# Forming the sums and differences of the mix weight rows on GpSimd in three passes instead of on VectorE in two

## What is computed

```python
mod_x = (silu_c @ w_ada[i] + b_ada[i])[:, None, :]          # six vectors of 2048: shift, scale, gate, twice
hx = _modulate(x, g_norm_mix[i], sh1, sc1)                   # rms norm, scale, shift
f = jnp.fft.fftn(hg, axes=(1, 3), norm='ortho').real         # over the tokens and over 4 groups of 512 channels
ox = f.reshape(b, n, d) @ w_out                              # the mix weights, 2048 x 2048
x = x + ga1 * ox
x = x + ga2 * _sq_relu_mlp(_modulate(x, g_norm_ffn[i], sh2, sc2), w_ffn_in[i], w_ffn_out[i])
return _rmsnorm(x, g_final)
```

## Time and profile before

| | |
|---|---|
| runs | 1649.15, 1648.82, 1647.47 us |
| the profiled execution: span from first to last instruction | 1651.0 us |
| TensorE busy | 1606.8 us (97%) |
| VectorE busy | 1266.2 us (77%) |
| ScalarE busy | 545.4 us (33%) |
| GpSimd busy | 16.8 us (1%) |
| mean granted TensorE clock | 0.992 of full |

### The profile page before, as it was taken

One profiled execution on the slowest core, in us unless ns is written; L12 is line 12 of the kernel. 1 busy time (PEld: TensorE's weight loads), 2 busy tenths in 40 slices (PEclk: granted clock), 3 DMA queues, 4 the chain that ended last, 5 costly groups with the idle time before them and its releaser, 6 DMA issues.

```text
span 1651.0 us, 18364 instructions
## 1 busy us (share of the span) xinstructions
PE 1606.8 (97%) x7009; PEld 1235.1 (75%) x7009; DVE 1266.2 (77%) x1168; ACT 545.4 (33%) x659; POOL 16.8 (1%) x30
## 2 busy tenths in 40 slices
PE   6989999999999999999999999999999999999997
PEld 5653332688888888888888888888888888888875
DVE  6758996748888888886868686868677777777878
ACT  5420002453333333333333333333333333333332
POOL 0000000100000000000000000000000000000000
PEclk9999999999999999999999999999999999999998
DMA  9999997924544444342323233323223323333352
GB/s 355 362 409 342 410 340 271 351 97 129 177 132 174 135 171 146 135 128 79 124 85 118 92 111 101 102 102 102 102 102 102 102 102 102 102 102 102 103 203 102
DMA packets 96970, 272.64 MB, mean 165 GB/s; under 512 B 4332, under 2 KB 5660, under 8 KB 85020
## 3 DMA queue, kind: packets, MB, share of 16 engines
q1 hardware_dynamic: 93664, 249.91, 42.3%
q0 software_dynamic: 3120, 22.07, 3.8%
q10 hardware_dynamic: 144, 0.07, 0.0%
HBM read 263.64 MB, written 8.39 MB: 165 GB/s over the span
## 4 chain that ended last, share of the span: by engine, by line
PE 87%; DVE 8%; DMA 3%; issue 2%; ACT 1%; SPq 0%; DVEq 0%; ACTq 0%
PE banks L1307 16%; PE banks L1308 16%; PE banks L1309 16%; PE banks L1613 11%; PE banks L1615 11%; PE banks L1617 11%; DMA raw<-in_w_ada 2%; DVE acc_s L823 1%; DVE acc_a L823 1%; DVE acc_b L1020 1%; PE banks L1534 1%; PE banks L1325 1%; DVE mixw L921 1%; DMA mixw<-in_w_mix 1%; PE banks L1450 1%
## 5 line engine op out<-in xcount | busy, mean ns | idle before, releaser
L1146 DVE TENSOR_TENSOR stp<-raw,stp 128x1024 fp32r<-128x1024 f32 x330 | 402.0, 1222 | 154.9 <-ACT stp L690 152.2
L690 ACT ACTIVATE stp<-raw 128x1024 fp32r<-128x1024 f32 x330 | 343.0, 1054 | 521.7 <-PE banks L1309 231.3
L1307 PE MATMUL banks<-acts,stp 128*128 128x512 f32 x1024 | 399.7, 390 | 0.0
L1308 PE MATMUL banks<-acts,stp 128*128 128x512 f32 x1024 | 398.4, 389 | 0.0
L1309 PE MATMUL banks<-acts,stp 128*128 128x512 f32 x1024 | 398.4, 389 | 0.0
L1613 PE MATMUL banks<-stp,hid 128*128 128x512 f32 x840 | 326.8, 389 | 0.0
L1615 PE MATMUL banks<-stp,hid 128*128 128x512 f32 x840 | 326.8, 389 | 0.0
L1617 PE MATMUL banks<-stp,hid 128*128 128x512 f32 x840 | 326.8, 389 | 0.0
L1167 DVE TENSOR_TENSOR dacc<-dacc,banks 128x1024 f32<-128x1024 f32 x202 | 245.5, 1215 | 14.2 <-PE banks L1617 14.2
L1309 PEld LDWEIGHTS banks<-acts,stp 128*128 128x128 f32 x1024 | 192.2, 188 | 40.0
L1307 PEld LDWEIGHTS banks<-acts,stp 128*128 128x128 f32 x1024 | 192.3, 188 | 39.8 <-DVE stp L1146 0.4
(11 more groups left out here) (190 smaller groups left out, 1227.1 us busy)
## 6 DMA issues: line engine op xcount, KB each, us to landing
raw<-in_w_ada SPq DMA_DIRECT2D x80, 1024.0 KB, 8.2
raw<-in_w_ffn_in SPq DMA_DIRECT2D x64, 1024.0 KB, 7.3
raw<-in_w_ffn_out SPq DMA_DIRECT2D x64, 1024.0 KB, 5.1
mixw<-in_w_mix SPq DMA_DIRECT2D x16, 1024.0 KB, 10.3
gate_w<-in_w_ada POOLq DMA_DIRECT2D x16, 1024.0 KB, 5.3
xres<-in_x SPq DMA_DIRECT2D x4, 1024.0 KB, 9.0
xmix_d<-xres POOLq DMA_DIRECT2D x4, 1024.0 KB, 12.7
xmix<-xmix_d SPq DMA_DIRECT2D x4, 1024.0 KB, 8.0
```

The lines of the kernel that those rows point to most:

```text
L690: nc.scalar.activation(stp[:, slot, 0, :, :], source.rearrange("p (a n) -> p a n", a=2), ACT.Copy).then_inc(w_hi, 1)
L1146: nc.vector.tensor_tensor(stp[:, slot, 1, :, :], source.rearrange("p (a n) -> p a n", a=2), stp[:, slot, 0, :, :].bitcast(F32), ALU.subtra ...
L1307: nc.tensor.matmul(bank, w_hi_ap, m_hi, start=first, stop=False)
L1308: nc.tensor.matmul(bank, w_hi_ap, m_lo, start=False, stop=False)
```

## The change

`mix_sums` moves from DVE to GpSimd. [...] A pass waits for the one before it (`w_sum`), and the first for the tile's load. GpSimd does all 16 units in one loop, after the memset of `acc_s` and its bias row's DMA, and ahead of the memset of `acc_a`. On DVE the two passes of each unit are gone, and ahead of the first `up_low` stands a wait for `w_lo` at 16, which keeps the semaphore's count in order.

```diff
-    AHEAD = UPDATED[-1] + 1
@@ gpsimd
+            def mix_sums(n):
+
+                tile = mixw[n % MIX_SLOTS]
+                pool.wait_ge(mix_full[n % MIX_SLOTS], 16 * (n // MIX_SLOTS + 1))
+                nc.gpsimd.tensor_tensor(tile[:, 2:4, :], tile[:, 0:2, :], tile[:, 2:4, :],
+                                        ALU.subtract).then_inc(w_sum, 1)
+                pool.wait_ge(w_sum, 2 * n + 1)
+                nc.gpsimd.tensor_tensor(tile[:, 0:2, :], tile[:, 0:2, :], tile[:, 0:2, :],
+                                        ALU.add).then_inc(w_sum, 1)
+                pool.wait_ge(w_sum, 2 * n + 2)
+                nc.gpsimd.tensor_tensor(tile[:, 0:2, :], tile[:, 0:2, :], tile[:, 2:4, :],
+                                        ALU.subtract).then_inc(w_lo, 1)
+
             for i, acc in enumerate((acc_s, acc_a)):
                 if i == 0:
                     pool.wait_ge(chan_sum, 2 * GROUPS)
                 else:
+                    for n in range(MU):
+                        mix_sums(n)
                     pool.wait_ge(col_sum, 2)
@@ vector
-            def mix_sums(n):
-                ...
-            mix_sums(0)
             shift_vector()
@@ vector, the loop over the units
-                if 1 <= n < AHEAD:
-                    mix_sums(n)
...
-                if n == AHEAD - 1:
-                    for later in range(AHEAD, MU):
-                        mix_sums(later)
...
+            dve.wait_ge(w_lo, MU)
+
             def up_low(m):
```

## The result

| | before | changed |
|---|---|---|
| median of the runs | 1648.99 us (4 runs, 1647.47 to 1650.82) | 1690.40 us (4 runs, 1688.76 to 1691.21) |
| span of the profiled execution | 1651.0 us | 1687.9 us |
| GpSimd busy | 16.8 us | 186.4 us |
| VectorE busy | 1266.2 us | 1303.9 us |

The ratio is 1.0247, 95% interval 1.0232 to 1.0261: the change makes the kernel slower by 41.4 us, where 52 had been forecast. Between the two profiled executions the difference is 36.9 us. The span of an execution is about 1.9 us shorter than its time (1687.9 against 1689.83 us for the changed kernel's profiled one), so the profiled execution of the kernel before was some 3.9 us longer than its median and the changed one 0.6 us shorter; that is the 4.5 us between 41.4 and 36.9.

A forecast was written before the change was run, and what follows sets the result against it. The prediction took PE as the bound, with DVE and DMA close. DVE's 93.3 us and POOL's 94.5 us in turn made 187.8 against 145.6, +52.0 including 9.8 at the start; 1648.8 + 52 gave 1701 us, range 1676 to 1726.

The forecast's parts named there:

- one after the other: DVE's two-SBUF-operand passes and POOL's reading passes alternate in the full stretch: +52.0 us, chance 0.52.
- What bounds the kernel: Stage from 131.4 to 277.1 us: PE first, sums of units 2 to 15 hidden behind its about 10 us a unit.
- A pass on POOL: One GpSimd sum pass over 1024 elements a partition: 2.25 us, between 1.80 and 2.70; 7.35 us a unit with gaps.
- The start: Unit 0 has no cover: its sums ready on POOL at 123.0 us, so PE starts 9.8 us later.
- the ISA instruction: Unnamed instruction opening POOL's loop, ahead of the passes: taken at 5.2 us, between nothing and 10.3.
- Do they disturb each other: Whether DVE's gemv-stage passes and POOL's passes of 14 units slow each other: from 0 to +52.0 us.
- the high end: Full stretch: DVE's 93.3 us plus POOL's 94.5 make 187.8 where there were 145.6; +52.0 us with the start.
- Costed at nothing: DVE passes with one operand in PSUM or only one operand, 10.1 us in all, can go beside POOL's.
- The end: Late tile of w_ada, unit 15: PE's wait and slow clock, 6.5 us, stay since its load follows DVE's last passes.
- Side by side: Rival: the two engines do not disturb each other; 9.8 us lost, 0.9 + 6.5 back, 1651 us; chance 0.22.
- Half way: Rival: path shared in small pieces, or POOL's passes fall partly into DVE's gaps; about 1676 us; chance 0.13.
- Worse than the sum: Rival: PE waits each unit, its clock falls, units at half clock outlast POOL's; over 1726 us; chance 0.05.

The follow-up runs named there:

- the version with unit 15 later: Kernel before, all sums on DVE, those of unit 15 moved behind the combination and update of column block 2: 1644.73 us, ratio 0.9958.
- the thirty passes: Kernel before plus thirty GpSimd passes of 128x1024 on a free scratch tile: 1696.14 us as two-operand adds, 1673.51 as copies, 1650.89 as memsets.
- the half passes: Changed kernel with each GpSimd pass of 128x1024 cut into two of 128x512: 1692.15 us, ratio 1.0249.

## Why the prediction was right, and by how much its terms were off

The forecast was 1701 us by the mechanism "one after the other", own range 1676 to 1726; measured 1690.4. The mechanism was right, sizes were not. The forecast of +52.0 stands against +41.4 between the medians and, between the profiles, +36.8 at the late tile. Step by step:

- **What bounds the kernel.** PE first, and it waits for no sums of units 2 to 15; but DVE's wait for the load of unit 15 reached PE through the late tile. Taking DVE's wait for unit 15 away gained 5.6 us; putting POOL's reading passes beside DVE cost 19 to 46 us, and in the changed kernel DVE was first. PE takes 9.6 us a unit, (270.80 - 136.28) / 14, since unit 15 begins at 270.80; the prediction's 10 came from a row in the middle of that unit. In turns a unit took 12.6 us (POOL's starts at 164.31 and 176.91).
- **A pass on POOL.** I took 2.25 us between 1.80 and 2.70; measured 2.36, 1.89 and 2.34, a mean of 2.20, and 6.74 us for a unit against 7.35. The middle of the bounds held.
- **The start.** 9.8 us forecast, 4.7 and then 5.0 measured. The term that failed is the ISA instruction, which I had priced at 5.2 us from the landing of a small DMA; 0.10 us lie between the DMA issue and the first pass. Without it the forecast for the start was 4.6. The Trainium skill, "GPSIMD Engine Reference", 2.1, has about 6 us for the first call of freshly loaded code; they do not show here (0.10 us).
- **Do they disturb each other.** Yes. The choice of the high end was right, but it could not be read from the rows before; it was a chance of 0.52. I had argued that a two-operand pass uses all of DVE's reading, which the rows could show, and that POOL takes part in the same path, which they could not. The rule of the Trainium skill, "SBUF — State Buffer", "Who interferes with whom", is what the runs show: GpSimd's reading and a DVE pass with two SBUF operands exclude each other (a gemv pass of 2.35 us takes 4.1), writing alone does not (0.95 us a memset, 2.35 a gemv pass), and the turn is a whole instruction.
- **The term that was mis-sized**: 93.3 + 94.5 = 187.8 us, where the stretch took 177.1. I added the durations of the passes. A gemv pass and a GpSimd pass together would be 2.35 + 2.20 = 4.55 us; measured were three such pairs in those 12.6 us, 4.20 each. So 0.35 us of each pair overlaps. Two of POOL's 42 passes, those that ended at 193.9 and 237.0 us, had their own 2.36 and 2.34 us beside DVE's passes from PSUM and cost DVE none of that; for the other 40 the overlap makes 14.0 us, an estimate from three pairs.
- **Costed at nothing, wrongly.** I said that passes with one operand can go beside POOL's. With the operand in PSUM they did (1221 ns before and after). The `TENSOR_SCALAR` passes from SBUF did not: 1.28 became 2.97, and the two halves 1.5 together became 3.6. The prediction's own figures spoke against it: it has one operand read at 1600 elements a microsecond and two at 1743, so this pass took nearly all the reading too, while the passes with one operand in PSUM take 1024 elements from SBUF in 1.22 us, 839 a microsecond. And what runs beside POOL still takes DVE's time: 2.8 us for the `TENSOR_SCALAR` passes and 7.3 for those from PSUM were missing in the 187.8, of which POOL's two passes above cover 4.7.
- **The end.** The late tile's wait stayed, as forecast (5.32 us now), since DVE remained its feeder: SP issued its load at 310.99 us, when the first of DVE's last three halves had ended (310.97); before, at 274.48 (about 274.45). That it would go with a DVE that is early is shown by the version with unit 15 later.
- **The rivals.** Side by side, 1651 us, is excluded by the result and by the thirty passes. Half way, 1676 us: the measured 1690.4 lies nearly in the middle between it and 1701, so the time alone would not decide; the half passes exclude sharing in small pieces. Its other half, that some of POOL's work falls where DVE does not need the path, is true of the two passes above. Worse than the sum: the clock's fall at PE's waits was real, but PE had time in hand, and the chain lay on DVE.

With these sizes the stretch is 187.8, less 2.2 for the shorter passes (42 of 2.20 against 2.25 us, 92.3 in all), less 14.0 for the overlap, plus 2.8, plus 7.3 - 4.7: 177.0 us, beside 177.1 measured. That it comes out to 0.1 us is partly luck, since the overlap is read from three pairs and DVE's own gaps are not counted by themselves. With the start at 5.0 instead of 9.8 us, the +52.0 become 36.4, beside 36.5 at the first `up_low` (313.59 against 277.08).

## What to carry to other kernels

Idle time of GpSimd is not free capacity while DVE works on SBUF: count each GpSimd pass that reads SBUF as time taken from DVE's passes that read two SBUF operands (or one, as the `TENSOR_SCALAR` here), about its duration less 0.35 us here, and use GpSimd for such passes only where DVE waits or works from PSUM, or for pure writing. When an engine's work is hidden behind another's, look for the one place where it is not: moving the sums of a single unit past a wait gained 5.6 us, while moving all of them to an idle engine lost 41 us.

## What the runs showed of the hardware that I had not expected

- A GpSimd pass whose two operands are the same tile (a + a) took 1.89 us, one with two different operands 2.34 to 2.36, at the same 128x1024.
- A `TENSOR_SCALAR` on DVE with one SBUF operand, 1.28 us for 128x2048, takes turns with GpSimd's reading as the two-operand passes do (2.97 us), although it reads one stream only.
- DVE's small copies, too: the copy into `shift` took 0.28 us before and 1.98 us in the changed kernel, beside GpSimd's second pass of unit 1.

```profile
125.71 0.29 DVE L928 COPY shift<-mods 128x256 f32<-128x256 f32 x1
125.92 1.98 DVE L928 COPY shift<-nyquist 128x256 f32<-128x256 f32 x1
```
